# The second norm of a block and the norm between two blocks: multiply the next phase's first two weight units by x times gain, and scale their accumulators by the root afterwards

## The reference, cut to what matters

```python
def _rmsnorm(x, g):
    y = x * lax.rsqrt(jnp.mean(jnp.square(x), axis=-1, keepdims=True) + EPS)
    return y * g

h = _rmsnorm(x, g_mix[l])
proj = h @ w_in[l]                     # first columns used: the conv branch's "glu", then na q, k, v, ...
...
x = x + mixed @ w_out[l]               # phase "out"
u = _depthwise_conv(_rmsnorm(x, g_ffn[l]) @ w_up[l], conv_w, conv_b)     # phase "up"
gate, up = jnp.split(u, 2, axis=-1)
x = x + (silu(gate) * up) @ w_down[l]  # phases "down0" and "down1"
```

## Time and profile before

| | |
|---|---|
| median of 3 runs | 2592.59 us (2591.53 to 2598.31) |
| profiled execution, own time | 2593.69 us |
| its span | 2591.9 us |
| PE busy | 2533.8 us, 98% of the span |
| DVE busy | 1656.5 us, 64% |
| ACT busy | 1295.6 us, 50% |
| POOL busy | 88.9 us, 3% |
| granted TensorE clock, mean | 0.995 |

### The profile page before, as it was taken

The page is one execution under the profiler, slowest core; times in us unless marked ns, Lnnn a source line. Parts: engine busy times, 40 slices in busy tenths (PEclk is TensorE's granted clock), DMA queues, the critical chain, the costliest instruction groups (busy, mean ns, idle before and its releaser), DMA issues.

```text
span 2591.9 us, 44766 instructions
## 1 busy us (share of the span) xinstructions
PE 2533.8 (98%) x18300; PEld 2229.4 (86%) x18300; DVE 1656.5 (64%) x2360; ACT 1295.6 (50%) x2086; POOL 88.9 (3%) x103
## 2 busy tenths in 40 slices
PE   7999999999999999999999999999999999999999
PEld 7999999999899888888876788888888888877999
DVE  6888786787887666364534577356576374645655
ACT  5555654456465566173335467154366173445443
POOL 2001100000100000000030000000000000010000
PEclk9999999999999999999999999999999999999999
DMA  8456766535775646444333336545446444453673
GB/s 240 138 156 195 189 181 211 183 132 159 211 199 158 203 127 175 120 135 130 113 92 115 111 112 174 145 116 150 116 118 175 125 131 137 123 163 108 186 209 110
DMA packets 613410, 393.48 MB, mean 152 GB/s; under 512 B 47303, under 2 KB 608949, under 8 KB 613108
## 3 DMA queue, kind: packets, MB, share of 16 engines
q1 hardware_dynamic: 610164, 383.14, 51.6%
q0 software_dynamic: 2176, 6.58, 1.1%
q10 hardware_dynamic: 896, 1.31, 0.2%
HBM read 389.94 MB, written 1.05 MB: 151 GB/s over the span
## 4 chain that ended last, share of the span: by engine, by line
PE 83%; DVE 8%; ACT 4%; DVEq 2%; issue 1%; POOL 1%; DMA 1%; ACTq 0%
PE acc L1077 11%; PE acc L1078 11%; PE acc L1079 11%; PE scores L1077 6%; PE scores L1078 5%; PE scores L1079 5%; PE scores L1140 3%; PE scores L1142 3%; PE scores L1141 3%; PE acc L1140 3%; PE acc L1142 3%; PE acc L1141 3%; DVEq L2186 2%; ACT prod L1672 1%; ACT raw L1672 1%
## 5 line engine op out<-in xcount | busy, mean ns | idle before, releaser
L1634 ACT ACTIVATE whi<-raw 128x2048 fp32r<-128x2048 f32 (+2 forms) x355 | 569.7, 1610 | 682.4 <-PE scores L1142 191.7
L2204 DVE TENSOR_TENSOR wlo<-raw,whi 128x2048 fp32r<-128x2048 f32 (+2 forms) x297 | 609.5, 2052 | 169.1 <-ACT whi L1634 165.5
L1077 PE MATMUL acc<-h,whi 128*128 128x512 f32 (+1 forms) x988 | 355.0, 359 | 5.1 <-DVE wlo L2204 2.9
L1078 PE MATMUL acc<-h,whi 128*128 128x512 f32 (+1 forms) x988 | 352.8, 357 | 0.0
L1079 PE MATMUL acc<-h,wlo 128*128 128x512 f32 (+1 forms) x988 | 352.6, 357 | 0.0
L1077 PE MATMUL acc<-h_hi,whi 128*128 128x256 f32 x1056 | 301.3, 285 | 3.1 <-DVE wlo L2204 2.8
L1078 PE MATMUL acc<-h_lo,whi 128*128 128x256 f32 x1056 | 294.9, 279 | 0.0
L1079 PE MATMUL acc<-h_hi,wlo 128*128 128x256 f32 x1056 | 294.7, 279 | 0.0
L1077 PE MATMUL scores<-h,whi 128*128 128x512 f32 (+1 forms) x608 | 219.5, 361 | 0.6 <-DVE wlo L2204 0.6
L1078 PE MATMUL scores<-h,whi 128*128 128x512 f32 (+1 forms) x608 | 219.2, 360 | 0.0
L1079 PE MATMUL scores<-h,wlo 128*128 128x512 f32 (+1 forms) x608 | 219.1, 360 | 0.0
(11 more groups left out here) (413 smaller groups left out, 5421.7 us busy)
## 6 DMA issues: line engine op xcount, KB each, us to landing
raw<-in_ffn_w_in_dram SPq DMA_DIRECT2D x176, 512.0 KB, 5.6
raw<-in_w_mod_dram SPq DMA_DIRECT2D x72, 1024.0 KB, 5.1
raw<-in_w_in_dram SPq DMA_DIRECT2D x62, 1024.0 KB, 5.1
raw<-in_w_up_dram SPq DMA_DIRECT2D x88, 512.0 KB, 5.1
raw<-in_ffn_w_out_dram SPq DMA_DIRECT2D x64, 704.0 KB, 4.8
raw<-in_w_down_dram SPq DMA_DIRECT2D x32, 704.0 KB, 4.6
raw<-in_w_out_dram SPq DMA_DIRECT2D x16, 1024.0 KB, 5.9
raw<-in_w_branch_dram SPq DMA_DIRECT2D x16, 512.0 KB, 6.1
```

Source lines behind the costliest of these rows:

```text
L1077: pe.matmul(bank, wh, hi[:, c0 + k, 0:width], start=(k == 0), stop=False)
L1078: pe.matmul(bank, wh, lo[:, c0 + k, 0:width], start=False, stop=False)
L1634: return act.activation(out_, in_, ACT.Copy, **kw)
L2204: dve.tensor_tensor(wlo[:, s % 2, 0:el], raw[:, slot, 0:el], f32(whi[:, s % 2, 0:el]), ALU.subtract).then_inc(s_lo, 1)
```

## The change

For the three gaps the first two units of the next phase no longer wait for the root. ACT writes `xg[0]` = round(x·gain) for each chunk right after it has squared it (`plain_hi`). `xg[1]`, the rest, is made by DVE (`plain_lo`), one instruction a chunk, for all chunks ahead of `glu` and for chunks 6 and 7 ahead of `up`; for chunks 0 to 5 ahead of `up` it is made by POOL, two instructions a chunk. PE runs unit 0 whole and then unit 1 whole out of `xg`, with the norm's sum put ahead of chunk 3 of unit 0 (`plain_units`), and the two modulation units behind unit 1. DVE multiplies the four finished accumulators by the root in place in PSUM (`norm_tiles`), two of them ahead of chunk 5 of the norm, two behind chunk 7; whoever reads them waits for `s_normed`. `h_hi` and `h_lo` are still made, for the third unit on, which waits for each chunk (`fresh`). The third unit's weights are split ahead of chunk 5. In `last_plain` the last square and the last `plain_hi` go ahead of both halves of the second unit's rounding. The banks of the phases `branch` and `out` are swapped: `out` now ends in `scores`, and unit 0 waits only for the tiles of `out` that lay in `acc`.

```diff
+PLAIN_STAT = 3
+PLAIN_TURN = 5
+POOL_LOWS = 6
...
+                xg = q("xg", [P, 2, DC, SEQ], F32R)
                 cstage = q("cstage", [P, 2, D])
+                xt = cstage[:, 0, 0:2 * SEQ].rearrange("p (b t) -> p b t", b=2)
...
         def pair_bank(j, q):
-            return (sp_[0], sp_[1], acc[0], acc[1])[q]
+            return (acc[0], acc[1], sp_[0], sp_[1])[q]
         def out_bank(j, m):
-            return (sp_, acc)[j % 2][m]
+            return (acc, sp_)[j % 2][m]
...
# GpSimd, behind its additions for the branches of layer l
+                for c in range(POOL_LOWS):
+                    k = POOL_LOWS * l + c
+                    pool.wait_ge(s_accfree, ph.t0 + c + 1)
+                    pool.tensor_scalar(xt[:, c % 2, :], x[:, c, :], pcol(("g_ffn", l), c), None, ALU.mult).then_inc(s_xt, 1)
+                    pool.wait_ge(s_xt, k + 1)
+                    pool.wait_ge(s_xhi, DC * plain_gap(f"1.{l}.up") + c + 1)
+                    pool.tensor_tensor(xg[:, 1, c, :], xt[:, c % 2, :], f32(xg[:, 0, c, :]), ALU.subtract).then_inc(s_xlo_pool, 1)
...
# TensorE
+            def plain_units(name, spec):
+                ph = by_name[name]
+                for e in range(2):
+                    pe.wait_ge(s_accfree, ph.t0 - 2 * (1 - e))
+                    for k in range(DC):
+                        if e == 0 and k < POOL_LOWS and name.endswith("up"):
+                            pe.wait_ge(s_xlo_pool, n("xlo_pool", 1))
+                        elif e == 0:
+                            pe.wait_ge(s_xlo, n("xlo", 1))
+                        if e == 0 and k == PLAIN_STAT:
+                            norm(spec)
+                        if e and k == 0:
+                            pe.wait_ge(s_lohalf, n("lohalf", 1))
+                        if k == 4 * e:
+                            pe.wait_ge(s_lo, ph.s0 + e + 1)
+                        for m in range(2):
...
+                            pe.matmul(bank, wh, xg[:, 0, k, :], start=(k == 0), stop=False)
+                            pe.matmul(bank, wh, xg[:, 1, k, :], start=False, stop=False)
+                            ins = pe.matmul(bank, wl, xg[:, 0, k, :], start=False, stop=(k == DC - 1))
...
             # unit(): the third unit of up, and naq
+                        if fresh and m == 0:
+                            pe.wait_ge(s_hl, n("hl", 1))
...
-                norm(norm_x(1, ("g_ffn", l), h1_hi, h1_lo))
+                plain_units(nm + "up", norm_x(1, ("g_ffn", l), h1_hi, h1_lo))
                 gap_mods(nm + "up")
-                first_units(nm + "up", h1_hi, h1_lo, SEQ, 1)
...
# ScalarE
+            def plain_hi(gain, c):
+                act.activation(xg[:, 0, c, :], x[:, c, :], ACT.Identity, scale=pcol(gain, c)).then_inc(s_xhi, 1)
+            def last_plain(spec, ph, gain):
+                act.wait_ge(s_accfree, ph.t0)
+                square(spec, DC - 1)
+                plain_hi(gain, DC - 1)
+                round_second(ph, 0)
+                round_second(ph, 1)
+                take_root(spec)
+            def third_unit(name):
+                return lambda e: round_next(name, 1, None) if e == PLAIN_TURN else None
...
                 # glu of layer 1
+                if l:
+                    act.wait_ge(s_normed, 4 * plain_gap(nm + "glu") + 4)
                 for m in range(2):
                     tile_out(ph.t0 + m, u1[:, m, CONV_PAD:CONV_PAD + SEQ], SEQ, scale=0.5).then_inc(s_accfree, 1)
...
                 # up
+                    if i is None and j < 2:
+                        act.wait_ge(s_normed, 4 * plain_gap(nm + "up") + 2 * j + 2)
                     act.wait_ge(s_acc, at(ph.t0 + 2, j, i, 2))
...
# VectorE
+            def plain_lo(name, gain, c):
+                dve.wait_ge(s_xhi, DC * plain_gap(name) + c + 1)
+                dve.scalar_tensor_tensor(xg[:, 1, c, :], x[:, c, :], pcol(gain, c), f32(xg[:, 0, c, :]), ALU.mult, ALU.subtract)\
+                   .then_inc(s_xlo, 1)
+            def norm_tiles(ph, e):
+                for m in range(2):
+                    dve.wait_ge(s_acc, ph.t0 + 2 * e + m + 1)
+                    bank = bank_of(ph, e, m, 4)[:, 0:SEQ]
+                    dve.tensor_tensor(bank, bank, rstd[:, 0:SEQ], ALU.mult).then_inc(s_normed, 1)
+            def scale_plain(name, spec):
+                ph = by_name[name]
+                def among(e):
+                    if e == PLAIN_TURN:
+                        norm_tiles(ph, 0)
+                        rest_next(name, 1, None)
+                rest_second(ph, 0)
+                flatten(spec)
+                rest_second(ph, 1)
+                scale_norm(spec, flat=True, between=among)
+                norm_tiles(ph, 1)
...
-                rest_second(by_name[nm + "up"], 0)
-                scale_norm(spec, second=by_name[nm + "up"])
+                for c in range(POOL_LOWS, DC):
+                    plain_lo(nm + "up", ("g_ffn", l), c)
+                scale_plain(nm + "up", spec)
                 mod_out(("gap", nm + "up"))
...
                         if h == 1 and j:
                             add_square(spec, j - 1)
+                            if l < DEPTH - 1:
+                                plain_lo(f"1.{l + 1}.glu", ("g_mix", l + 1), j - 1)
                         dve.wait_ge(s_acc, ph.t0 + j + 1)
```

More of the change, by code:

```diff
@@ L559, in build @@
         s_half = sem("s_half")
+        s_xhi = sem("s_xhi")
+        s_xt = sem("s_xt")
+        s_xlo = sem("s_xlo")
+        s_xlo_pool = sem("s_xlo_pool")
+        s_normed = sem("s_normed")
         s_acc = sem("s_acc")
@@ L816, in ctx_bank, with plain_gap @@
             return down_bank(ph, 4) if ph.n == DC else sp_[0]
+        def plain_gap(name):
+            return ("1.0.up", "1.1.glu", "1.1.up").index(name)
         def next_unit(ph, j):
@@ L1048, in parted, with unit @@
                     ins.then_inc((s_accx, s_acc)[seg], 1)
-            def unit(name, j, i, hi, lo, width, weights, c0=0, ring=2, upto=None, free=None):
+            def plain_units(name, spec):
[15 more added lines that the diff above has]
+                            bank = bank_of(ph, e, m, 4)[:, 0:SEQ]
+                            cols = slice(k * 256 + m * P, k * 256 + m * P + P)
+                            wh, wl = (w[:, (ph.s0 + e) % 2, cols] for w in (whi, wlo))
+                            pe.matmul(bank, wh, xg[:, 0, k, :], start=(k == 0), stop=False)
+                            pe.matmul(bank, wh, xg[:, 1, k, :], start=False, stop=False)
+                            ins = pe.matmul(bank, wl, xg[:, 0, k, :], start=False, stop=(k == DC - 1))
+                            if k == DC - 1:
+                                ins.then_inc(s_acc, 1)
+            def unit(name, j, i, hi, lo, width, weights, c0=0, ring=2, upto=None, free=None, fresh=False):
                 ph = by_name[name]
@@ L1059, in unit @@
                     if ring == 4 and ph.tiles == DC:
-                        if m % 2 == 0 and (j or m >= 4):
+                        if m % 2 == 0:
                             pe.wait_ge(s_accfree, t - 6 if j else ph.t0)
@@ L1317, in _ @@
                 if l:
-                    norm(norm_x(1, ("g_mix", l), h1_hi, h1_lo))
+                    plain_units(nm + "glu", norm_x(1, ("g_mix", l), h1_hi, h1_lo))
                     gap_mods(nm + "glu")
-                first_units(nm + "glu", h1_hi, h1_lo, SEQ, 1)
+                else:
+                    first_units(nm + "glu", h1_hi, h1_lo, SEQ, 1)
                 if l == 0:
@@ L1347, in _ @@
                     else:
-                        unit(nm + name, 0, None, h1_hi, h1_lo, SEQ, plain(256))
+                        unit(nm + name, 0, None, h1_hi, h1_lo, SEQ, plain(256), fresh=l > 0 and name == "naq")
                 pe.wait_ge(s_rpbm, 4 * (l + 1))
@@ L1445, in _ @@
                     unit(nm + "out", j, None, h1_hi, h1_lo, SEQ, plain(256), ring=4)
-                norm(norm_x(1, ("g_ffn", l), h1_hi, h1_lo))
+                plain_units(nm + "up", norm_x(1, ("g_ffn", l), h1_hi, h1_lo))
                 gap_mods(nm + "up")
-                first_units(nm + "up", h1_hi, h1_lo, SEQ, 1)
-                for j, i in steps(pe, FC, 2):
+                for j, i in steps(pe, FC, 3):
                     if i is None and j < 2:
                         continue
-                    unit(nm + "up", j, i, h1_hi, h1_lo, SEQ, plain(256), ring=4)
+                    unit(nm + "up", j, i, h1_hi, h1_lo, SEQ, plain(256), ring=4, fresh=i is None and j == 2)
                 for h in range(2):
@@ L1732, in take_root, with down_squares @@
                                ACT.Sqrt, bias=eps[:, 0:1], scale=spec["scale"]).then_inc(s_root, 1)
-            def down_squares(name, spec):
+            def down_squares(name, spec, gain=None):
                 ph = by_name[name]
@@ L1743, in down_squares, with out_squares @@
                         square(spec, j - 1)
-            def out_squares(name, spec):
+                        if gain:
```

(43 more changed lines are left out.)

2 lines of the change are left out of this document (added).

## The result

| | before | after |
|---|---|---|
| median of 8 runs each, us | 2592.28 (2590.59 to 2598.31) | 2600.39 (2598.9 to 2603.51) |
| profiled execution, own time / span | 2593.69 / 2591.9 | 2600.31 / 2598.4 |
| granted TensorE clock, mean | 0.995 | 0.997 |

The ratio is 1.0028, with a 95% interval of 1.002 to 1.0037: slower by 8.1 us between the medians and by 7.3 us by the ratio (5.2 to 9.6), small, but clear of no change. The forecast was 2600.4.

A forecast was written before the change was run, and what follows sets the result against it. PE, busy 98% of the span, was taken as the bound, with DVE's path equally long in the `up` gaps. Terms 1.7 (`glu`) + 2.5 (`up`) + 3.6 (clock) gave +7.8 us, median 2600.4; range 2594 to 2606.

The forecast's parts named there:

- PE's gain turned into a wait: Ahead of the third `up` unit: PE ready near 269.5, but the unit starts about 274.3, held by DVE.
- DVE's path in `up`, +0.4 a gap: DVE in each `up` gap: 0.8 + 1.4 us added work and 1.4 new waits, less 3.2 us removed waits.
- GpSimd's contention, +0.85 a gap: During `out`: POOL instructions delay DVE, so the last chunk of x comes 0.85 us late; range 0 to 2.4.
- the full rule: DVE with two SBUF inputs shut out until POOL's instruction ends: two `up` gaps cost +5.6 us instead of +2.5.
- The `glu` gap, +1.7: `naq` starts at 471.1 against 469.44, behind `norm_tiles`, ACT's copies, table load and first Tanh; range 0.4 to 2.5 us.
- The clock, 3 x 1.2: PE's long waits drop the clock to half: 1.2 us lost a gap, +3.6 in all; above 1.7 each, 5.1.
- The sum: Whole kernel: 1.7 + 2.5 + 3.6 = +7.8 us, median 2600.4.
- (a): Rival: DVE path as computed, but the clock stays up or falls inside the waits: +4.2 us, 2596.8; chance 0.25.
- (b): Rival: POOL locks DVE out for each whole instruction, last chunk of x 2.4 us late: +10.9, 2603.5; chance 0.14.
- (c): Rival: DVE's path does not bind, PE keeps 4.5 us a gap, 13.5 in all: 2579; chance 0.06.

The follow-up runs named there:

- the early taps: Changed kernel with unit 0's three taps in the `up` gaps put right behind the third unit's rounding, ahead of norm chunks 5 to 7: 2599.68 us, ratio 1.0028.
- the filled kernel: Changed kernel with unread matmuls behind the modulation units in PE's waits, 36 in each `up` gap and 48 in `glu`: 2594.93 us, ratio 1.0006.
- the early table: Changed kernel with a one-column Tanh in `glu` ahead of ACT's wait for the accumulators, so its table loads in that wait: 2602.66 us, ratio 1.0035.
- the kernel with all three edits: Changed kernel with unread matmuls (8 per `up` gap, 38 in `glu`), Tanh's table loaded in ACT's wait and unit 0's taps moved earlier: 2593.65 us, ratio 1.0004.

## Why the prediction came out right, step by step

**PE's gain turned into a wait.** Right. PE was ready 4.85 us ahead of the third unit (predicted 4.8, from 269.5 to 274.3), and 273.94 became 274.16 (predicted 274.3). The windows of DVE show that the second path was full, with 16.94 of its 18.56 us as work, and the early taps that another order does not open it.

**DVE's path in `up`, +0.4 a gap.** Measured -0.1 (18.67 to 18.56). The added work was sized well: 2.57 us against 2.2. The waits fell by 2.68 where I had 3.2 - 1.4 = 1.8 us: I left out the 0.43 us in `mod_out` and the short gaps between instructions, which other work now fills. The term was 0.5 us a gap too large.

**GpSimd's contention, +0.85 a gap.** This is the term that failed. The last chunk of x begins 0.54 us after the last matmul of `out`, where before it was 0.49. In other executions it was later (1.11 us in the filled kernel, with gaps of 19.78), so the cost is 0 to 0.6 us a gap and changes from one execution to the next. DVE's `wlo` in `out` took 2.29 us, where I expected 0.2 to 0.5 us more. What contention there was fell on the additions of squares (1.41 instead of 0.94), in front of slack, and on GpSimd itself, whose timeline in the kernel after has the same two instructions alone and beside DVE's `wlo`:

```profile
240.81 1.76 POOL L968 TENSOR_TENSOR xg<-cstage,xg 128x256 fp32r<-128x256 f32 x1 [1.41 <-ACT xg L1775]
...
243.59 0.73 POOL L968 TENSOR_TENSOR xg<-cstage,xg 128x256 fp32r<-128x256 f32 x1
244.30 0.93 POOL L965 TENSOR_SCALAR cstage<-x,par 128x256 f32<-128x256 f32 x1
...
250.84 3.05 POOL L965 TENSOR_SCALAR cstage<-x,par 128x256 f32<-128x256 f32 x1
```

The Trainium skill, page "SBUF — State Buffer", section "Who interferes with whom", has the later of the two shut out until the first is done. This trace agrees on both sides: GpSimd's 1.76 and 3.05 us began beside a `wlo` and ended 0.6 to 0.7 us after it, and DVE's additions at 248.46 took 0.47 us more than their 0.94 beside a subtraction of GpSimd that ended at 248.96. But GpSimd was mostly the later one, and it had time: its last instruction ended at 256.6, and PE came to that chunk no sooner than 30 matmuls of 0.118 us behind 255.07. The +5.6 us that the prediction put on the full rule took DVE to be the later one throughout; no run shows that cost.

**The `glu` gap, +1.7.** Measured +1.5, of which the early table gave back 1.25.

**The clock, 3 x 1.2.** Measured 1.15, 2.56 and 1.06, 4.8 us in all; filling the waits made the kernel 5.5 us faster, 3.6 of them in the gaps. For `up` the size was right. At `naq` the half clock lasted twice as long as in the one row I had the earlier trace rows, so its price doubled; my upper bound of 1.7 a gap was too low for that. The trace of the kernel before could have warned of it, with a longer stretch near its start:

```profile
13.10:23.40 10.30, 7.10 (x30) 0.50 1.02 321
```


**The sum.** 0.0 + 1.5 + 4.8 = 6.3 us against 6.5 of the spans; predicted 7.8. The mechanism was right; that the forecast of 2600.4 fell within 0.01 us of the median was luck, as several errors met: DVE and GpSimd 2.5 us too dear, the clock 1.2 us too cheap, `glu` 0.2 too dear, and the medians lay another 1.6 us further apart than the two profiled spans. With 6.8 us of half clock, as in the kernel with only the `up` gaps changed, the fourth unit starts 27.59 us after `out` and not 26.31, so the clock term alone can move the sum by 1.3 us a gap from one execution to the next.

**The rivals.** (a), a harmless clock, is refuted by the filled kernel. (b), GpSimd locking DVE out, is refuted: the last chunk of x was no more than 0.6 us late. (c), DVE's path not the bound, is refuted by the third unit's start and by the early taps.

## What to carry to other kernels

Before taking a dependency off the busiest engine, add up the work of the next engine over the same gap: here its path of 18.67 us was as long as PE's, and paying for the shortcut with 2.6 us of DVE work used up just the idle time it freed. Many short waits turned into one long one can cost more than they did, since the clock can fall behind it (1.06 to 2.56 us a gap here); matmuls that nobody reads, put into the wait, show what that is worth. Where a wait is moved onto an engine, look for a table load queued behind it.

## What the runs showed that I had not expected

- The half clock came in stretches of 3.4 us, two or three of them, and which it was changed between executions of like gaps: 3.4, 6.8 and 3.4 us in the kernel after, 6.8 in all three with the early table. The start moved too: just ahead of the third unit's first matmul (273.9 and 274.16), or 2.7 us ahead of it (271.9 and 274.58). After a wait of 3.0 us for the fourth unit the clock fell in some gaps and stayed at 1.00 in others (the first gap of the kernel with all three edits).
- The filled kernel had none in its gaps, although PE still stood still for 1 us ahead of the third unit.
- GpSimd's multiplication by a scalar took 3.05 us beside DVE's `wlo` and 0.93 alone, while DVE's halves of `wlo` beside such work took 1.22 to 1.41. Spans on GpSimd are rough, but the next instruction in its queue moved with it.
